# Forget-gate columns and indexer keys computed by feature and turned back; FoX's second log-forget product on the second key tile alone

## The chip, the cores and the metric

The program runs on one core of one Trainium2 chip, as one launch. The time is in device microseconds. The engines are TensorE (PE in the rows, with its weight loads as PEld), VectorE (DVE), ScalarE (ACT), GpSimd (POOL) and SyncE (SP), which issues most of the DMAs. Each engine works through its own instructions in order, and they wait for each other by semaphores.

## What is computed

A sequence of 256 tokens with 1024 features goes through two layers of a first block (feed-forward, a mixer of three kinds, cross attention to a memory, feed-forward) and then two layers of a second block (short convolution, sparse attention with an indexer, pooling, gates). What bears on this case is below.

```python
def first_block(...):                       # for each of DEPTH = 2 layers
    x = x + 0.5 * swiglu(rms_norm(x, ffn1_norm[l]), ffn1_w_in[l], ffn1_w_out[l])
    z = rms_norm(x, mix_norm[l]) @ mix_w_in[l]
    z_fox, z_moba, z_rwkv = jnp.split(z, [FOX_IN, FOX_IN + MOBA_IN], axis=-1)
...
def fox_mixer(z, f_bias, q_gain, k_gain):
    q, k, v, f = jnp.split(z, [FOX_WIDTH, 2 * FOX_WIDTH, 3 * FOX_WIDTH], axis=-1)   # f: 4 columns
    log_f = jax.nn.log_sigmoid(f + f_bias)
    # scores: q k^T / 8 + c[query] - c[key], c = cumsum(log_f) over tokens, causal, softmax
...
def rwkv7_mixer(z, ...):
    r, k, v, w_lo, a_lo, g_lo = jnp.split(zf, ...)       # low: 64 + 64 + 160 columns
    w_raw = w0 + jnp.tanh(w_lo) @ w2
    a = jax.nn.sigmoid(a0 + a_lo @ a2)
...
def sparse_attention_mixer(q, k, v, gate, iq, ik, iw, ...):  # second block
    iq = apply_rope(iq.reshape(B, S, IDX_HEADS, IDX_DIM), cos, sin)
    ik = apply_rope(ik[:, :, None, :], cos, sin)[:, :, 0, :]  # ik: 64 columns, iw: 8 columns
    score = einsum(relu(iq ik^T / 8), iw) / sqrt(8)           # picks top keys for each query
```

## The kernel before

**Weights.** All weights come in one stream of units of 128x1024 fp32 numbers (512 KB). SP loads unit u into one of four raw buffers as soon as VectorE has split unit u - 4. ScalarE (`act_split`, L315) rounds the unit to `whi`, once TensorE has used unit u - 4, and VectorE (`dve_split`, L324) writes the rest to `wlo`. TensorE multiplies each pair of operands in three matmuls (high by high, high by low, low by high), so one unit of 512 columns is 4 groups of 3 matmuls of 512 columns (`pe_unit`, L342 to L344), with the activations as the stationary operand and the weights moving: 128 tokens come out on partitions, features along the free axis. `pe_unit_turned` (L350) does it the other way: the weights are the stationary operand, all 256 tokens move, and the features come out on partitions.

**Mixer, low columns.** `pe_rw_low` works through four units. Of each, for two slices `kk` of 128 input features, `blocks` gives three outputs by feature (128, 96 and 64 partitions by 256 tokens, L367 to L369), and `beside` gives the four forget-gate columns by token (two tiles of 128 tokens by 4 columns, L362 to L364). ScalarE's `act_rw_low` then copies the three blocks to `LM` with a scale each (L884 to L886) and the 2x4 forget columns to `Z` (L887); VectorE's `dve_rw_low` adds the shifted tokens (L902). TensorE meanwhile does the first two units of group `z` 1, then `pe_rw_lora` (L928, L932), then two more, `pe_rw_cum`, and group 2.

**Forget gates.** `dve_at_tables` part 0 (L1507, L1509) prepares the gates, `act_at_tables` (L1522, L1524) takes the exponential and logarithm, part 1 the sign and factor. In `pe_at_scores`, FoX's logits of one head get one product for the queries and keys and then, for each token tile `st` up to the query tile, a product of the log gates `LN` (broadcast to 128 stationary columns) with the table `cum` (L1587). `cum` for `st` = 1 is zero for keys 0 to 127, since tokens of the second tile add nothing to the sums of the first.

**Second block.** `pe_block2` begins with the groups iq (four units), ik (one unit of 8 slices of 72 columns: 64 key columns and 8 head weights), k (four units). `pe_unit_keys` makes 72 columns by token in banks 2 and 0: per token tile 8 slices of 3 matmuls (L2360 to L2362). ScalarE's `act_group` scales them into `ikw` (L2374, L2375). VectorE turns iq and then ik by their angles (`dve_sp_index`, L2390 to L2398, L2411), with one `dve_split` between them, and TensorE's `pe_sp_index` transposes both (L745) behind the third unit of k. The groups take three pairs of banks in turn, each waiting for the copies of those before.

## Time and profile before

| | before |
|---|---|
| median of 3 runs | 1896.34 us |
| lowest, highest | 1893.74 us, 1907.27 us |
| the profiled execution | 1899.43 us |
| its span | 1898.1 us |
| TensorE busy | 1857.7 us (98%) |
| VectorE busy | 1165.2 us (61%) |
| ScalarE busy | 927.7 us (49%) |
| mean granted TensorE clock | 0.991 |

The span is the time from the first to the last recorded instruction; 1.3 us of the profiled execution lie around it. A matmul's row has its start and a modelled length; since matmuls overlap, what one costs is the distance from its start to the next one's start. The granted clock is 1.00 at 2.4 GHz and 0.50 at 1.2 GHz.

### The profile page before, as it was taken

How to read it: one execution, taken by the hardware profiler on the slowest of the kernel's cores; microseconds unless marked ns; L12 is line 12 of the kernel's file. 1: busy time of each engine (PE TensorE's matmuls, PEld its weight loads, DVE VectorE, ACT ScalarE, POOL GpSimd, SP SyncE). 2: the span in 40 equal slices, each digit the busy share in tenths (PEclk: the TensorE clock that was granted, in tenths of full speed). 3: DMA queues.
4: the chain of work that ended last, by engine and by line, in shares of the span. 5: the costliest groups of instructions: out<-in, count | busy, mean ns of one | idle time of the engine just before them, and what ended most of it. 6: DMA issues, size and time to landing. Idle time of an engine off the chain costs nothing.

```text
span 1898.1 us, 28284 instructions
## 1 busy us (share of the span) xinstructions
PE 1857.7 (98%) x11756; PEld 1565.4 (82%) x11756; DVE 1165.2 (61%) x1645; ACT 927.7 (49%) x1409; POOL 93.6 (5%) x59
## 2 busy tenths in 40 slices
PE   7999999999999999999999989999999999999999
PEld 6888888887888888888888878888888888888887
DVE  5555477765655565554677656555588548597556
ACT  5444474234544454445642355444455554556553
POOL 0000010040000000000100400000010000000000
PEclk9999999999999999999999999999999999999999
DMA  6655442023555566554420235655554456454454
GB/s 241 249 183 175 145 156 78 25 79 112 168 189 188 177 191 248 188 176 143 155 71 25 79 111 187 205 184 174 165 168 159 152 188 210 151 166 156 161 186 141
DMA packets 83616, 299.19 MB, mean 158 GB/s; under 512 B 9632, under 2 KB 10784, under 8 KB 83232
## 3 DMA queue, kind: packets, MB, share of 16 engines
q1 hardware_dynamic: 79328, 287.87, 45.8%
q10 hardware_dynamic: 3840, 8.03, 1.2%
q8 instruction: 93, 1.52, 0.3%
q0 software_dynamic: 320, 1.48, 0.2%
q14 instruction: 35, 0.29, 0.0%
HBM read 296.30 MB, written 1.05 MB: 157 GB/s over the span
## 4 chain that ended last, share of the span: by engine, by line
PE 94%; DVE 4%; issue 0%; ACT 0%; DMA 0%; POOL 0%; ACTq 0%; DVEq 0%
PE ps L342 24%; PE ps L344 24%; PE ps L343 24%; PE ps L367 2%; PE ps L369 2%; PE ps L368 2%; PE ps L808 1%; PE ps L1184 1%; PE ps L566 1%; PE ps L1187 1%; DVE wlo L324 1%; PE ps L2500 1%; PE ps L1175 1%; PE ps L1587 1%; PE ps L780 1%; DVE a_lo L420 1%
## 5 line engine op out<-in xcount | busy, mean ns | idle before, releaser
L324 DVE TENSOR_TENSOR wlo<-raw,whi 128x1024 fp32r<-128x1024 f32 (+1 forms) x546 | 663.3, 1222 | 423.0 <-ACT whi L315 422.0
L315 ACT ACTIVATE whi<-raw 128x1024 fp32r<-128x1024 f32 (+1 forms) x546 | 573.0, 1053 | 512.2 <-PE ps L344 468.2
L342 PE MATMUL ps<-whi,a_hi 128*128 128x512 f32 x1696 | 677.0, 399 | 5.8 <-DVE a_lo L1874 1.8
L344 PE MATMUL ps<-whi,a_lo 128*128 128x512 f32 x1696 | 663.8, 391 | 0.0
L343 PE MATMUL ps<-wlo,a_hi 128*128 128x512 f32 x1696 | 662.8, 391 | 0.0
L342 PEld LDWEIGHTS ps<-whi,a_hi 128*128 128x128 f32 x1696 | 320.2, 189 | 76.0 <-DVE a_lo L1874 2.3
L344 PEld LDWEIGHTS ps<-whi,a_lo 128*128 128x128 f32 x1696 | 319.7, 189 | 68.7
L343 PEld LDWEIGHTS ps<-wlo,a_hi 128*128 128x128 f32 x1696 | 320.5, 189 | 62.8
L342 PE MATMUL ps<-whi,h_hi 128*128 128x512 f32 x320 | 124.9, 390 | 0.0
L344 PE MATMUL ps<-whi,h_lo 128*128 128x512 f32 x320 | 124.6, 389 | 0.0
L343 PE MATMUL ps<-wlo,h_hi 128*128 128x512 f32 x320 | 124.5, 389 | 0.0
L367 PE MATMUL ps<-a_hi,whi 128*128 128x256 f32 (+2 forms) x304 | 88.7, 292 | 0.0
L369 PE MATMUL ps<-a_hi,wlo 128*128 128x256 f32 (+2 forms) x304 | 85.9, 282 | 0.0
L368 PE MATMUL ps<-a_lo,whi 128*128 128x256 f32 (+2 forms) x304 | 85.8, 282 | 0.0
L344 PEld LDWEIGHTS ps<-whi,h_lo 128*128 128x128 f32 x320 | 60.1, 188 | 12.5
L343 PEld LDWEIGHTS ps<-wlo,h_hi 128*128 128x128 f32 x320 | 60.1, 188 | 12.3
L342 PEld LDWEIGHTS ps<-whi,h_hi 128*128 128x128 f32 x320 | 60.1, 188 | 12.3
L588 ACT ACTIVATE arena<-ps,small 128x256 f32<-128x256 f32 x88 | 36.9, 470 | 67.2 <-PE ps L344 67.2
L631 DVE SCALAR_TENSOR_TENSOR arena<-ps,small,arena 128x256 f32<-128x256 f32 x88 | 38.5, 479 | 40.0 <-ACT arena L588 40.0
L497 POOL TENSOR_TENSOR small<-small,minus_half 128x2 f32<-128x2 f32 x10 | 7.0, 700 | 1057.3 <-DVE small L490 703.8
L367 PEld LDWEIGHTS ps<-a_hi,whi 128*128 128x128 f32 (+2 forms) x304 | 56.8, 187 | 0.7 <-issue 0.3
L368 PEld LDWEIGHTS ps<-a_lo,whi 128*128 128x128 f32 (+2 forms) x304 | 56.9, 187 | 0.2
(317 smaller groups left out, 1847.3 us busy)
## 6 DMA issues: line engine op xcount, KB each, us to landing
raw<-stream SPq DMA_DIRECT2D x546, 512.0 KB, 3.4
arena<-rows ACTq DMA_DIRECT2D x2, 1026.0 KB, 12.6
arena<-mem ACTq DMA_DIRECT2D x2, 1024.0 KB, 8.7
arena<-lora ACTq DMA_DIRECT2D x2, 768.0 KB, 6.1
arena<-rows ACTq DMA_DIRECT2D x2, 512.0 KB, 4.9
const_tables<-consts POOLq DMA_DIRECT2D x1, 901.0 KB, 4.9
arena<-band POOLq DMA_DIRECT2D x1, 544.0 KB, 4.0
x_res<-x SPq DMA_DIRECT2D x1, 512.0 KB, 3.7
```

What stands on the lines that cost most here:

```text
L315: self.split_hi.mark(act.activation(self.weights(self.whi, u), self.weights(self.raw, u), ACT.Copy), u)
L324: self.split_lo.mark(dve.tensor_tensor(self.weights(self.wlo, u), self.weights(self.raw, u), self.weights(self.whi, u).bitcast(F32), ALU.s ...
L342: pe.matmul(out, a_h, hi, start=start, stop=False, skip_group_check=True)
L343: pe.matmul(out, a_h, lo, start=False, stop=False, skip_group_check=True)
L344: last = pe.matmul(out, a_l, hi, start=False, stop=True, skip_group_check=True)
L367: pe.matmul(out, hi, self.AHI[:, kt, :], start=first and kt == 0, stop=False, skip_group_check=True)
L368: pe.matmul(out, hi, self.ALO[:, kt, :], start=False, stop=False, skip_group_check=True)
L369: last = pe.matmul(out, lo, self.AHI[:, kt, :], start=False, stop=True, skip_group_check=True)
L420: self.turned_lo.mark(dve.scalar_tensor_tensor(self.ALO[:, place, :], self.bank(banks[k % 4], S), gain[:, k:k + 1], self.AHI[:, place, :]. ...
L566: ins = pe.transpose(self.bank(banks[kk])[:, t * P:(t + 1) * P], self.h_buffer(j)[:, t, kk * P:(kk + 1) * P], self.c("ident"))
L588: self.silu.mark(act.activation(self.SG[:, t, :], self.bank((2 if j == 1 else 4) + t, 256), ACT.Silu, scale=self.rs(0, t)), key, j, t)
L631: self.h_ready.mark(dve.scalar_tensor_tensor(self.h_buffer(j)[:, t, :], self.bank((2 if j == 1 else 4) + t)[:, 256:512], self.rs(0, t), se ...
```

## The change

Three edits. The layouts of the weights in memory stay as they are.

1. The forget gates' four columns become rows 64 to 67 of the third block by feature (68 partitions instead of 64), and `beside` is gone. `act_rw_low` copies 68 rows to `LM`, the four with a scale of 1. Behind `pe_rw_lora` TensorE transposes the four rows back to tokens, for two tiles, and ScalarE copies them to `Z` behind the LoRA's sigmoids. VectorE's two small gate instructions stand behind `dve_at_norm`. Group 2 of `z` waits for the copy too.
2. In `pe_at_scores` the product for key tile `st` writes columns from `st` x 128 on alone.
3. The indexer's keys and head weights are computed by feature (72 partitions by 256 tokens in bank 3), copied to `sIKT` by ScalarE, transposed back by TensorE behind the first unit of k, and scaled into `ikw` by ScalarE behind one more split.

```diff
@@ -349,4 +349,3 @@
 
-    def pe_unit_turned(self, n, blocks, beside=()):
-
+    def pe_unit_turned(self, n, blocks):
@@ -358,8 +357,2 @@
             kt = 2 * n + kk
-            for out, c, w, first, t in beside:
-                hi, lo = self.whi[i][:, kk, c:c + w], self.wlo[i][:, kk, c:c + w]
-                a_h, a_l = self.AHI[:, kt, t * P:(t + 1) * P], self.ALO[:, kt, t * P:(t + 1) * P]
-                pe.matmul(out, a_h, hi, start=first and kt == 0, stop=False, skip_group_check=True)
-                pe.matmul(out, a_h, lo, start=False, stop=False, skip_group_check=True)
-                pe.matmul(out, a_l, hi, start=False, stop=True, skip_group_check=True)
             for out, c, w, first in blocks:
@@ -860,4 +853,3 @@
         self.pe_unit_turned(n, [(self.bank(0)[:, S:2 * S], 96, P, True), (self.bank(0)[0:96, 0:S], 0, 96, False),
-                                (self.bank(1)[0:64, 0:S], 224, 64, False)],
-                            [(self.bank(1)[:, S + 4 * t:S + 4 * t + 4], 288, 4, t == 0, t) for t in range(NT)])
+                                (self.bank(1)[0:68, 0:S], 224, 68, True)])
@@ -885,5 +877,3 @@
         m.mark(act.activation(M[:, 1, :], self.bank(0)[:, S:2 * S], ACT.Copy, scale=self.pv(PV_OML, 1)), "low", l, 1)
-        m.mark(act.activation(M[0:64, 2, :], self.bank(1)[0:64, 0:S], ACT.Copy, scale=self.pv(PV_OML, 2, 64)), "low", l, 2)
-        m.mark(act.activation(self.Z[:, :, ZF:ZF + 4], self.bank(1)[:, S:S + 8].rearrange("p (t h) -> p t h", t=NT),
-                              ACT.Copy), "forget", l)
+        m.mark(act.activation(M[0:68, 2, :], self.bank(1)[0:68, 0:S], ACT.Copy, scale=self.pv(PV_OML, 2, 68)), "low", l, 2)
         act.wait_ge(*self.rw_dve("low", l, 0))
@@ -897,3 +887,3 @@
         for i, w, src, need in ((0, 96, self.bank(0)[0:96, 0:S], ("low", l, 1)), (1, P, self.bank(0)[:, S:2 * S], None),
-                                (2, 64, self.bank(1)[0:64, 0:S], ("forget", l))):
+                                (2, 64, self.bank(1)[0:64, 0:S], ("low", l, 2))):
             if need is not None:
@@ -934,2 +924,6 @@
         self.rw_pe.mark(ins, "a", l)
+        for t in range(NT):
+            ins = pe.transpose(self.bank(1)[:, S + 4 * t:S + 4 * t + 4], self.LM[64:68, 2, t * P:(t + 1) * P],
+                               self.c("ident")[64:68, 64:68])
+        self.rw_pe.mark(ins, "forget", l)
@@ -943,2 +937,5 @@
             m.mark(act.activation(self.AT[:, i, :], self.half((6, 7), i), ACT.Sigmoid, bias=self.pv(PV_A0, i)), "a", l, i)
+        act.wait_ge(*self.rw_pe("forget", l))
+        m.mark(act.activation(self.Z[:, :, ZF:ZF + 4], self.bank(1)[:, S:S + 8].rearrange("p (t h) -> p t h", t=NT),
+                              ACT.Copy), "forget", l)
@@ -1586,4 +1583,4 @@
                 for st in range(qt + 1):
-                    ins = pe.matmul(out, self.LN[:, st, h:h + 1].to_broadcast([P, P]),
-                                    self.c("cum")[:, st * S:st * S + nk], start=False, stop=st == qt,
+                    ins = pe.matmul(out[:, st * P:nk], self.LN[:, st, h:h + 1].to_broadcast([P, P]),
+                                    self.c("cum")[:, st * S + st * P:st * S + nk], start=False, stop=st == qt,
                                     skip_group_check=True)
@@ -1943,3 +1940,3 @@
         pe, banks = self.nc.tensor, self.ZB[g]
-        for sem, value in {1: [], 2: [self.rw_dve("low", l, 2)], 3: self.z_done(l, 1)}[g]:
+        for sem, value in {1: [], 2: [self.rw_dve("low", l, 2), self.rw_act("forget", l)], 3: self.z_done(l, 1)}[g]:
             pe.wait_ge(sem, value)
@@ -2191,5 +2188,3 @@
         self.dve_rw_low(l)
-        self.dve_split(3)
-        self.dve_at_tables(l, 0)
-        self.dve_split(1)
+        self.dve_split(4)
         self.dve_z(l, 1)
@@ -2197,2 +2192,3 @@
         self.dve_at_norm(l, True)
+        self.dve_at_tables(l, 0)
         self.dve_split(1)
@@ -2320,3 +2316,3 @@
         first = 4 * g - 3 * (g > 1)
-        dst = self.ikw if name == "ik" else self.slot[name] if name in self.slot else self.mg[name[2]][name[1]]
+        dst = None if name == "ik" else self.slot[name] if name in self.slot else self.mg[name[2]][name[1]]
         return self.unit2(self.layer, "p") + first, ((2 * g) % 3, (2 * g + 1) % 3), dst
@@ -2333,3 +2329,3 @@
                 pe.wait_ge(*self.z_act1("p", l, self.GROUPS[g - 2]))
-            if g > 0:
+            if g > 0 and name != "k":
                 late = [self.z_act("p", l, self.GROUPS[g - 1])]
@@ -2340,3 +2336,3 @@
         if name == "ik":
-            self.pe_unit_keys(banks, late)
+            self.pe_unit_keys()
             return
@@ -2345,3 +2341,3 @@
 
-    def pe_unit_keys(self, banks, late):
+    def pe_unit_keys(self):
@@ -2350,16 +2346,32 @@
         pe.wait_ge(*self.split_lo(u))
-        hi, lo = self.weights(self.whi, u), self.weights(self.wlo, u)
-        for t in range(NT):
-            if t:
-                for sem, value in late:
-                    pe.wait_ge(sem, value)
-            out = self.bank(banks[t], 72)
-            for kt in range(8):
-                a_h, a_l = self.AHI[:, kt, t * P:(t + 1) * P], self.ALO[:, kt, t * P:(t + 1) * P]
-                h, low = hi[:, kt * 72:(kt + 1) * 72], lo[:, kt * 72:(kt + 1) * 72]
-                pe.matmul(out, a_h, h, start=kt == 0, stop=False, skip_group_check=True)
-                pe.matmul(out, a_h, low, start=False, stop=False, skip_group_check=True)
-                last = pe.matmul(out, a_l, h, start=False, stop=kt == 7, skip_group_check=True)
+        hi, lo, out = self.weights(self.whi, u), self.weights(self.wlo, u), self.bank(3)[0:72, 0:S]
+        for kt in range(8):
+            h, low = hi[:, kt * 72:(kt + 1) * 72], lo[:, kt * 72:(kt + 1) * 72]
+            pe.matmul(out, h, self.AHI[:, kt, :], start=kt == 0, stop=False, skip_group_check=True)
+            pe.matmul(out, h, self.ALO[:, kt, :], start=False, stop=False, skip_group_check=True)
+            last = pe.matmul(out, low, self.AHI[:, kt, :], start=False, stop=kt == 7, skip_group_check=True)
         self.unit_used.mark(last, u)
 
+    def act_keys(self, l):
+        act = self.nc.scalar
+        self.layer = l
+        act.wait_ge(*self.unit_used(self.group("ik")[0]))
+        self.sp_act.mark(act.activation(self.sIKT[0:72, :], self.bank(3)[0:72, 0:S], ACT.Copy), "ik", l)
+
+    def pe_keys_turn(self, l):
+
+        pe = self.nc.tensor
+        pe.wait_ge(*self.sp_act("ik", l))
+        for t in range(NT):
+            ins = pe.transpose(self.bank(3)[:, S + 72 * t:S + 72 * (t + 1)], self.sIKT[0:72, t * P:(t + 1) * P],
+                               self.c("ident")[0:72, 0:72])
+        self.sp_pe.mark(ins, "ik", l)
+
+    def act_keys_out(self, l):
+        act = self.nc.scalar
+        act.wait_ge(*self.sp_pe("ik", l))
+        for t, m in enumerate((self.z_act, self.z_act1)):
+            m.mark(act.activation(self.ikw[:, t, :], self.bank(3)[:, S + 72 * t:S + 72 * (t + 1)], ACT.Copy,
+                                  scale=self.rs(0, t)), "p", l, "ik")
+
     def act_group(self, l, name):
@@ -2369,3 +2381,3 @@
         func = ACT.Sigmoid if name[0] == "mg" else self.FUNCS[name] if name in self.FUNCS else ACT.Copy
-        act.wait_ge(*self.unit_used(unit + (0 if name == "ik" else 3)))
+        act.wait_ge(*self.unit_used(unit + 3))
         if name == "ag":
@@ -2846,4 +2858,6 @@
         self.pe_group(l, "ik", 0)
-        for n in range(3):
-            self.pe_group(l, "k", n)
+        self.pe_group(l, "k", 0)
+        self.pe_keys_turn(l)
+        self.pe_group(l, "k", 1)
+        self.pe_group(l, "k", 2)
         self.pe_sp_index(l)
@@ -2940,4 +2954,6 @@
         self.act_split(1)
-        self.act_group(l, "ik")
-        self.act_split(3)
+        self.act_keys(l)
+        self.act_split(1)
+        self.act_keys_out(l)
+        self.act_split(2)
         self.act_sp_index(l)
```

What TensorE does in the low columns, from the first unit on, is, before the change (L362 to L364 are the forget columns, L367 to L369 the blocks):

```order
L362 MATMUL ps<-whi,a_hi 128x4
L363 MATMUL ps<-wlo,a_hi 128x4
L364 MATMUL ps<-whi,a_lo 128x4
L362 MATMUL ps<-whi,a_hi 128x4
L363 MATMUL ps<-wlo,a_hi 128x4
L364 MATMUL ps<-whi,a_lo 128x4
L367 MATMUL ps<-a_hi,whi 128x256
L368 MATMUL ps<-a_lo,whi 128x256
L369 MATMUL ps<-a_hi,wlo 128x256
L367 MATMUL ps<-a_hi,whi 96x256
L368 MATMUL ps<-a_lo,whi 96x256
L369 MATMUL ps<-a_hi,wlo 96x256
```

and with the change, where the lines L360 to L362 are now those of the blocks:

```order
L360 MATMUL ps<-a_hi,whi 128x256
L361 MATMUL ps<-a_lo,whi 128x256
L362 MATMUL ps<-a_hi,wlo 128x256
L360 MATMUL ps<-a_hi,whi 96x256
L361 MATMUL ps<-a_lo,whi 96x256
L362 MATMUL ps<-a_hi,wlo 96x256
L360 MATMUL ps<-a_hi,whi 68x256
L361 MATMUL ps<-a_lo,whi 68x256
L362 MATMUL ps<-a_hi,wlo 68x256
L360 MATMUL ps<-a_hi,whi 128x256
```

The six matmuls of 4 columns are gone and the third block has 68 stationary columns.

At the keys of the second block, behind the last matmul of iq, TensorE has before the change 48 of these (here the first 6):

```order
L344 MATMUL ps<-whi,a_lo 128x512
L2360 MATMUL ps<-whi,a_hi 128x72
L2361 MATMUL ps<-wlo,a_hi 128x72
L2362 MATMUL ps<-whi,a_lo 128x72
L2360 MATMUL ps<-whi,a_hi 128x72
L2361 MATMUL ps<-wlo,a_hi 128x72
L2362 MATMUL ps<-whi,a_lo 128x72
```

and with the change 24 of these (here the first 4):

```order
L344 MATMUL ps<-whi,a_lo 128x512
L2350 MATMUL ps<-a_hi,whi 72x256
L2351 MATMUL ps<-a_lo,whi 72x256
L2352 MATMUL ps<-a_hi,wlo 72x256
L2350 MATMUL ps<-a_hi,whi 72x256
```

The moving operand went from 72 weight columns to 256 tokens. Between the first unit of k (12 matmuls, the last 3 here) and the second stands the turn with the change, two transposes of L2366; before, the two units followed each other directly:

```order
L342 MATMUL ps<-whi,a_hi 128x512
L343 MATMUL ps<-wlo,a_hi 128x512
L344 MATMUL ps<-whi,a_lo 128x512
L2366 MATMUL ps<-const_tables,arena 128x72 x2
L342 MATMUL ps<-whi,a_hi 128x512
```

Two transposes are added there, 12 matmuls of 512 columns behind the last of the keys.

ScalarE, from the copies of iq on, before the change:

```order
L2374 ACTIVATE arena<-ps,small 128x512
L2375 ACTIVATE arena<-ps,small 128x512
L315 ACTIVATE whi<-raw 128x1024
L2374 ACTIVATE arena<-ps,small 128x72
L2375 ACTIVATE arena<-ps,small 128x72
L315 ACTIVATE whi<-raw 128x1024 x3
L751 ACTIVATE arena<-ps 128x4x128 x2
```

and with the change, L2359 being the copy by feature and L2374 the two scaled copies by token:

```order
L2386 ACTIVATE arena<-ps,small 128x512
L2387 ACTIVATE arena<-ps,small 128x512
L315 ACTIVATE whi<-raw 128x1024
L2359 ACTIVATE arena<-ps 72x256
L315 ACTIVATE whi<-raw 128x1024
L2374 ACTIVATE arena<-ps,small 128x72 x2
L315 ACTIVATE whi<-raw 128x1024 x2
L744 ACTIVATE arena<-ps 128x4x128 x2
```

One of the three splits stands now between the first copy and the two others.

## Rows read from the trace of the kernel before

**Rows 1.** Page, parts 1 and 4: busy time by engine; chain by engine

```profile
PE 1857.7 (98%) x11756; PEld 1565.4 (82%) x11756; DVE 1165.2 (61%) x1645; ACT 927.7 (49%) x1409; POOL 93.6 (5%) x59
PE 94%; DVE 4%; issue 0%; ACT 0%; DMA 0%; POOL 0%; ACTq 0%; DVEq 0%
```

**Rows 2.** Waits of PE, whole span: line, what was waited for, total us, times, longest

```profile
PE ps L404 <- DMA x_res<-x: 9.5, 1, 9.5
```

**Rows 3.** Stretches of PE: us, busy (instructions), granted clock, DMA share, GB/s

```profile
208.16:222.04 13.88, 13.88 (x124) 1.00 0.36 115
870.87:884.75 13.88, 13.88 (x124) 1.00 0.34 115
1352.63:1358.37 5.74, 5.74 (x49) 0.92 0.72 221
1358.37:1364.39 6.02, 6.02 (x16) 0.51 0.41 139
1630.56:1637.61 7.05, 7.05 (x50) 0.74 0.70 214
1637.61:1640.97 3.36, 3.36 (x9) 0.54 0.05 18
```

**Rows 4.** Timeline of PE: start us, length us, line, tile, form, count

```profile
210.76 0.27 PE L368 MATMUL ps<-a_lo,whi 128*128 128x256 f32 x1
211.57 0.28 PE L369 MATMUL ps<-a_hi,wlo 128*64 128x256 f32 x1
...
279.25 0.28 PE L367 MATMUL ps<-a_hi,whi 128*128 128x256 f32 x1
283.21 0.28 PE L367 MATMUL ps<-a_hi,whi 128*128 128x256 f32 x1
```

**Rows 5.** Timeline of PE, narrow key matmuls, and 24 wide ones' first and last

```profile
222.04 0.40 PE L342 MATMUL ps<-whi,a_hi 128*128 128x512 f32 x1
227.28 0.40 PE L344 MATMUL ps<-whi,a_lo 128*128 128x512 f32 x1
...
1357.13 0.28 PE L2362 MATMUL ps<-whi,a_lo 128*128 128x72 f32 x1
1357.24 0.28 PE L2360 MATMUL ps<-whi,a_hi 128*128 128x72 f32 x1
```

**Rows 6.** Timeline of PE, four turns between feature-side matmuls

```profile
267.86 0.60 PE L745 MATMUL ps<-const_tables,arena 128*128 128x128 f32 x4
268.22 0.36 PE L367 MATMUL ps<-a_hi,whi 128*128 128x256 f32 x1
268.42 0.28 PE L368 MATMUL ps<-a_lo,whi 128*128 128x256 f32 x1
```

**Rows 7.** Timeline of PE in FoX's scores, first and second query tile

```profile
274.99 0.49 PE L1587 MATMUL ps<-const_tables,small 128*128 128x128 f32 x2
275.41 0.48 PE L1583 MATMUL ps<-arena 64*128 64x128 f32 x2
...
287.35 1.13 PE L1587 MATMUL ps<-const_tables,small 128*128 128x256 f32 x4
288.41 0.70 PE L1583 MATMUL ps<-arena 64*128 64x256 f32 x2
```

**Rows 8.** Timeline around block 2's keys, layer 0; in brackets idle before, releaser

```profile
1358.60 0.32 ACT L2374 ACTIVATE arena<-ps,small 128x72 f32<-128x72 f32 x1 [3.50 <-PE ps L2362]
1360.11 1.23 DVE L324 TENSOR_TENSOR wlo<-raw,whi 128x1024 fp32r<-128x1024 f32 x1
1362.31 0.36 DVE L2411 COPY small<-arena 128x128 f32<-128x128 f32 x2
1369.40 1.03 PE L745 MATMUL ps<-const_tables,arena 128*128 128x128 f32 x8
```

**Rows 9.** Timeline of ACT and DVE behind the LoRA step, layer 0

```profile
234.34 1.06 ACT L315 ACTIVATE whi<-raw 128x1024 fp32r<-128x1024 f32 x1 [1.42 <-PE ps L344]
244.36 1.23 DVE L324 TENSOR_TENSOR wlo<-raw,whi 128x1024 fp32r<-128x1024 f32 x1 [3.20 <-ACT whi L315]
```

## What the change does to the time: the prediction

> **What bounds the kernel now.** I read the page first: TensorE is busy for 1857.7 of 1898.1 us, and 94% of the chain that ended last is its own work, 4% VectorE's [rows 1]. The list of TensorE's waits comes next: its longest entry is the 9.5 us at the start for the load of x [rows 2], which no edit touches. So a microsecond of matmuls taken out is a microsecond of the end, as long as nothing that TensorE then meets earlier is late. What a matmul costs is therefore the distance between two starts, and I looked for it in the timeline, at every place that the change touches, and beside it at the granted clock of the same stretches. There the reader is to see two different things. In the low columns of both layers TensorE runs 13.88 us at a full clock [rows 3]. At the keys of the second block it stays busy throughout, and still the granted clock falls: 0.92 in the keys of layer 0 and 0.51 in the 6.02 us of wide matmuls behind them, 0.74 and 0.54 in layer 1 [rows 3]. The narrow key matmuls cost 0.11 us each at the full clock though they move only 72 columns [rows 5].
>
> **Part 1, the forget columns.** One layer's low stretch has eight slices of 15 matmuls: 6 of 4 columns and 9 of 256. The nine stay, one third of them with 68 stationary columns instead of 64. A 256-column matmul costs (211.57 - 210.76) / 7 = 0.116 us in this very stretch, with 64 to 128 stationary columns, and (283.21 - 279.25) / 33 = 0.120 us where all have 128 [rows 4]. I take 0.118: 72 of them are 8.50 us. The stretch shrinks from 13.88 by 5.38 us, in two layers by 10.8 us, with the two ends 10.5 and 11.1. The 48 removed per layer thus cost 0.112 us each, as much as one of 256 columns.
>
> What comes instead are two transposes per layer of 4 rows. The trace has no such small ones; the nearest are four of 128 columns: 0.36 us for four, and the next matmul's distance is 0.20 instead of 0.12 us [rows 6]. Two are 2 x 0.09 + 0.08 = 0.26 us. Low end nothing, since the next matmul may cover them, high end 0.6 us. They read what ScalarE and VectorE had to finish for the LoRA product directly ahead of them, so they wait for nothing new. The copy to Z moves on ScalarE behind the LoRA's sigmoids, where ScalarE then idles for 1.42 us before its next split [rows 9]; one small copy fits. VectorE's two gate instructions move behind the norm, where VectorE idles for 3.20 us [rows 9]. ScalarE's logarithm wants them only two splits later. Group 2 waits for the copy, but two units of weights and the cumulative sums lie between. I cost all this at nothing; if the cover were gone it would be the copy's own few tenths.
>
> The faster stretch also asks for weights sooner. A low unit is used up in 18 x 0.118 = 2.1 us instead of 3.5, and each use releases one split on ScalarE (1.06 us) and one on VectorE (1.23 us) [rows 9]. Both fit into 2.1 us, and the first unit of the next group is split 2.3 us behind the first low unit, when three low units, 6.4 us, are still to run. The transfers have room: the stretch uses 36% of the DMA engines [rows 3].
>
> **Part 2, FoX.** With 128 columns the log-gate product costs 275.41 - 274.99 = 0.42 us, with 256 columns (288.41 - 287.35) / 2 = 0.53 us [rows 7]. Four heads in two layers are 8 of them: 8 x 0.11 = 0.9 us. The lower end is 0, the upper one half of the wide product's cost, 8 x 0.265 = 2.1 us. I take the difference of the rows.
>
> **Part 3, the keys.** Now 48 narrow matmuls, then 24 of 256 columns with 72 stationary ones, 24 x 0.118 = 2.83 us. In layer 0 the keys take 5.74 us and the next 6.02 us hold the starts of 14 wide matmuls at half clock [rows 3] (the count in the row is 16 because two reach in). At the full clock a wide one costs (227.28 - 222.04) / 23 = 0.228 us [rows 5], 14 are 3.19 us. So 11.76 us become 2.83 + 3.19 = 6.02 and 5.7 us are saved. In layer 1 the keys take 7.05 and the next 8 wide ones 3.36 us [rows 3]; 10.41 become 2.83 + 1.82 = 4.65, again 5.8 us. Together 11.5 us. Of this 2 x (48 x 0.111 - 2.83) = 5.0 us is for fewer matmuls and 6.5 us for the clock. That the clock falls because of the narrow matmuls is my reading: both falls come during them, without any idle time. The low stretch, where the 4-column matmuls alternate with 256-column ones, keeps 1.00 [rows 3].
>
> The turn back is priced as above, 0.26 us per layer. It waits for ScalarE's copy of the keys. Layer 0 in the new order: keys end at 1352.6 + 2.8 = 1355.5, and the first unit of k keeps TensorE for 12 x 0.228 = 2.7 us. ScalarE is idle then (3.50 us before its old copy) [rows 8] and has 2.7 us for one copy, so I expect no wait. Behind the turn come two more units of k, and TensorE is at the index transposes at 1355.5 + 36 x 0.228 + 0.3 = 1364.0 instead of 1369.40 [rows 8]. It does 8 transposes of iq first (0.9 us) and then wants ik. VectorE's line does not move: it is at its split at 1360.11 and finishes ik at 1362.31 + 0.36 = 1362.7 [rows 8]. The slack before the ik transposes falls from some 7.6 to 2.2 us, but it stays. This is the step next in line to be late. Queued behind ScalarE's new wait for the turn are two splits, which need units of k that TensorE has not used by then anyway.
>
> **The sum.** 10.8 + 11.5 + 0.9 - 4 x 0.26 = 22.1 us. The profiled execution took 1899.43 us, so its like should take 1877.3 us. The median of the three runs, 1896.34, is 3.1 us lower; carried over, the forecast is 1874.2 us.
>
> **Rivals.** *The clock falls all the same.* The fall may belong to this place and not to the narrow matmuls. Then the 6.5 us stay and the gain is 15.6 us: 1880.7 us. Against it speaks that the other feature-side stretches hold the full pace (0.120 us through 33 distances) [rows 4]. Chance 0.12. The Trainium skill has such a rule, in "TensorE: Matmul & The Clock Gate", section "HAM oscillation": the clock is lost in idle gaps between bursts of matmuls. By that rule narrow matmuls without a gap lose nothing, and the trace disagrees, since the clock went to 0.51 with TensorE busy for all of the 6.02 us.
>
> *A wait takes the place of the work.* If VectorE's line at the keys ends later than I read, TensorE stands at the index transposes, and in the worst case arrives as late as now: 11.0 us of the gain go, 1885.2 us. It begins to count when VectorE is 2.2 us later. Against it: VectorE's chain there needs nothing later than before except ik itself. Chance 0.08.
>
> *Slower than before.* The new turned stretches or the arrival at new phases could bring further falls of the clock. One fall costs 6.02 - 3.19 = 2.8 us [rows 3]. It takes eight more of them than now to lose the 22.1 us, and 15 to be over 1% slower: 1915 us or more. For it speaks only that stationary blocks of 68 and 72 columns do not occur now in those stretches; those of 64 and 96 do, at full clock. Chance 0.02.
>
> **How the numbers follow.** The forecast has 0.78. Its own spread comes from the ends above (low columns ±0.3, FoX -0.9 to +1.2, turns -1.4 to +1.0), from falls of the clock elsewhere, of 2.8 us each, that may begin or end differently when all behind shifts, and from the three runs, which lie between 1893.74 and 1907.27. The range is 1868 to 1886 us: it takes in both smaller gains, and beyond it lie the last case and the tails. About 1% is what a measurement of this kernel can tell from no change; faster by over 1% means under 1877.4 us. The forecast is 3 us below that bound, so three quarters of its 0.78 count as faster, 0.58; the other quarter and the two smaller gains are within 1%, 0.40; slower has 0.02.
>
> **What would show it.** In the profile after: 72 matmuls in each low stretch in 8.4 to 8.7 us at clock 1.00; 24 key matmuls in 2.8 to 2.9 us and wide ones at 0.228 us behind them with clock 1.00, where now it falls; two turns at about 0.26 us each without idle time before them; 0.42 us for the second log-gate product; and no wait of TensorE at the index transposes. The prediction is wrong if the clock still falls behind the keys, if the 68- or 72-column blocks cost clearly over 0.12 us, or if new waits of several us stand in TensorE's list.

## The result, and the profile after

The changed kernel takes 1889.37 us (median of 11 executions, 1885.75 to 1892.29); the kernel before, timed beside it, 1904.02 us (1893.74 to 1908.95). The ratio is 0.9948, with a 95% interval of 0.9933 to 0.9964: faster by half a percent, within the 1% in which the prediction put 0.40. A repetition in a later session (e12) gave 0.9934 (0.9916 to 0.9953). The forecast of 1874.2 us was 15 us too low, and the result lies above its range. The medians differ by 14.7 us and the two profiled executions by 13.6 (1899.43 to 1885.86), where 22.1 were expected. The other half of the 15 us is the starting point: the forecast set out from 1896.34, the median of three executions of the kernel before, and the median of eleven is 1904.02.

Page of the kernel after, parts 1 and 4, and below it the first two entries of the list of waits of PE (line, what was waited for, total us, times, longest), against [rows 1] and [rows 2]:

```profile
PE 1844.4 (98%) x11620; PEld 1552.9 (82%) x11620; DVE 1164.7 (62%) x1645; ACT 928.3 (49%) x1411; POOL 93.6 (5%) x59
PE 94%; DVE 4%; issue 0%; ACT 0%; DMA 0%; POOL 0%; ACTq 0%; DVEq 0%
```

```profile
PE ps L397 <- DMA x_res<-x: 9.4, 1, 9.4
PE ps L839 <- DVE arena L832: 6.5, 2, 3.3
```

TensorE is busy for 13.3 us less, the chain is the same 94%, and no wait is new or longer. Now the places that the change touches. Stretches of PE of the kernel after (us, busy (instructions), granted clock, DMA share, GB/s): the low columns of both layers, the keys of layer 0, what follows them up to the index transposes, and the keys of layer 1 with what follows; against [rows 3]:

```profile
206.96:215.50 8.54, 8.54 (x76) 1.00 0.46 138
868.11:876.64 8.53, 8.53 (x75) 1.00 0.45 142
1350.21:1353.03 2.82, 2.82 (x25) 1.00 0.64 208
1353.03:1361.42 8.39, 8.39 (x40) 1.00 0.55 183
1625.30:1636.00 10.70, 10.70 (x56) 1.00 0.57 186
```

Timeline of PE, the two turns with the matmuls behind, and FoX's second query tile (start us, length us, line, tile, form, count), against [rows 6] and [rows 7]:

```profile
224.70 0.28 PE L926 MATMUL ps<-const_tables,arena 4*128 4x4 f32 x2
224.91 0.50 PE L342 MATMUL ps<-whi,a_hi 128*128 128x512 f32 x1
...
1355.77 0.29 PE L2366 MATMUL ps<-const_tables,arena 72*128 72x72 f32 x2
1355.86 0.48 PE L342 MATMUL ps<-whi,a_hi 128*128 128x512 f32 x1
1356.18 0.39 PE L343 MATMUL ps<-wlo,a_hi 128*128 128x512 f32 x1
```

```profile
281.02 0.92 PE L1584 MATMUL ps<-const_tables,small 128*128 128x256 f32 x4
281.87 0.70 PE L1580 MATMUL ps<-arena 64*128 64x256 f32 x2
```

All of it came as forecast: 8.54 us for 72 matmuls (8.50 expected), 2.82 for the keys (2.83), clock 1.00 behind them in both layers, 0.21 us for the forget turn, 0.09 + (0.32 - 0.23) = 0.18 for the keys' turn. FoX's pair of products takes 281.87 - 281.02 = 0.85 us for 1.06. So the gain was made, and something gave part of it back. Three stretches that ran at full clock before do not now:

```profile
321.00:327.80 6.80, 6.80 (x61) 0.50 0.00 0
368.80:372.20 3.40, 3.40 (x62) 0.50 0.04 14
942.20:955.90 13.70, 13.70 (x57) 0.50 0.00 1
```

The longest of them is in FoX's scores of the second query tile, layer 1. Timeline of PE there, before and then after; the two have the same instructions in the same order, but for the narrower second log-forget product of part 2. L1583 and L1587 of before are L1580 and L1584 of after:

```profile
949.44 0.70 PE L1583 MATMUL ps<-arena 64*128 64x256 f32 x2
950.06 1.13 PE L1587 MATMUL ps<-const_tables,small 128*128 128x256 f32 x4
```

```profile
940.53 1.08 PE L801 MATMUL ps<-arena 128*128 128x64 f32 x8
941.54 0.70 PE L1580 MATMUL ps<-arena 64*128 64x256 f32 x2
942.17 1.60 PE L1584 MATMUL ps<-const_tables,small 128*128 128x256 f32 x4
943.70 1.22 PE L1580 MATMUL ps<-arena 64*128 64x256 f32 x2
944.85 1.43 PE L1584 MATMUL ps<-const_tables,small 128*128 128x256 f32 x3
```

In after the first L1580 pair of this stretch still takes 942.17 - 941.54 = 0.63 us, as before (0.62); the next takes 944.85 - 943.70 = 1.15, with no idle time between the rows. The whole stretch, from the transposes of the first tile's probabilities through the spread of the lengths, before and then after, in both layers:

```profile
283.57:295.38 11.81, 11.81 (x87) 1.00 0.14 47
946.28:958.09 11.81, 11.81 (x87) 1.00 0.13 47
```

```profile
277.24:288.19 10.95, 10.95 (x86) 1.00 0.14 51
938.39:955.50 17.11, 17.11 (x87) 0.61 0.09 33
```

Layer 0 runs it at full clock and 0.86 us faster, which is part 2's work; layer 1 takes 17.11 us, 6.2 more than layer 0.

**One split for all runs.** Every execution has its span and its mean granted clock, and the low level is half of the full one. So span x (1 - clock) estimates the time lost to low clock, and span x clock the time that the same work takes at full clock. The estimate is good to about 2 us. The mean clock has three digits, which is 1 us, and the loss comes out a little too high: the stretch of the scores, 11.81 us at 1.00 and 18.15 at 0.62 (below), became 6.3 us longer, where the split says 18.15 x 0.38 = 6.9. It gives for the kernel before 1879.8 us of work and 20.5 us lost (mean of the 29 executions beside e1 to e4; 13 to 27 us lost), and for the changed kernel 1861.8 and 25.9 us (11 executions; 22.6 to 28.4).

In the other sessions the kernel before lost 16.6 to 21.3 us in the mean, with the same work within 0.5 us, so a difference in loss of a few us between sessions is not a finding. The work fell by 18.0 us and the loss rose by 5. The forecast had 15.6 us less work and 6.5 us less loss. Three executions stand apart and are left out of work and loss below, those of e3 and e14 of the medians too: one each of e2 (clock 0.936 at 1907.28 us, which by the split would be 122 us lost), e3 (10507.77 us) and e14 (3076.41 us); why they were so I do not know.

### The profile page after: what moved, and what is told of

Same layout as the page of the kernel before. It is cut to its first block, busy times and chain, and to the rows that moved or that the text cites. A ratio compares the mean times of both kernels' runs of the same rounds, so it can differ in the third digit from the quotient of the medians.

```text
span 1884.5 us, 28014 instructions
## 1 busy us (share of the span) xinstructions
PE 1844.4 (98%) x11620; PEld 1552.9 (82%) x11620; DVE 1164.7 (62%) x1645; ACT 928.3 (49%) x1411; POOL 93.6 (5%) x59
## 4 chain that ended last, share of the span: by engine, by line
PE 94%; DVE 4%; issue 0%; ACT 0%; DMA 0%; POOL 0%; ACTq 0%; DVEq 0%
PE ps L342 24%; PE ps L344 24%; PE ps L343 24%; PE ps L360 2%; PE ps L362 2%; PE ps L361 2%; PE ps L801 1%; PE ps L1181 1%; PE ps L559 1%; PE ps L1184 1%; DVE wlo L324 1%; PE ps L1172 1%; PE ps L1584 1%; PE ps L773 1%; PE ps L2512 1%; PE ps L1580 1%
## 5 line engine op out<-in xcount | busy, mean ns | idle before, releaser
L360 PE MATMUL ps<-a_hi,whi 128*128 128x256 f32 (+2 forms) x304 | 87.7, 288 | 0.0
L362 PE MATMUL ps<-a_hi,wlo 128*128 128x256 f32 (+2 forms) x304 | 85.9, 283 | 0.0
L342 PEld LDWEIGHTS ps<-whi,h_hi 128*128 128x128 f32 x320 | 60.1, 188 | 12.3
L360 PEld LDWEIGHTS ps<-a_hi,whi 128*128 128x128 f32 (+2 forms) x304 | 56.9, 187 | 0.9 <-issue 0.5
```

The source lines that it names most:

```text
L342: pe.matmul(out, a_h, hi, start=start, stop=False, skip_group_check=True)
L360: pe.matmul(out, hi, self.AHI[:, kt, :], start=first and kt == 0, stop=False, skip_group_check=True)
L362: last = pe.matmul(out, lo, self.AHI[:, kt, :], start=False, stop=True, skip_group_check=True)
```

## The experiments

All were timed in 5 rounds beside the kernel before. "Useless matmuls" are extra products of 512 columns into a bank that the next product starts afresh, at the head of the first wide unit behind the low columns; TensorE is at full clock there and each costs 0.23 us.

| run | what | median us | ratio to before (95%) | work us | lost us, mean (range) |
|---|---|---|---|---|---|
| after | the change | 1889.37 | 0.9948 (0.9933 to 0.9964) | 1861.8 | 25.9 (22.6 to 28.4) |
| e1_low | part 1 alone | 1902.67 | 1.0006 (0.9986 to 1.0026) | 1868.3 | 32.8 (24.6 to 40.0) |
| e2_fox | part 2 alone | 1902.98 | 0.9995 (0.9976 to 1.0014) | 1877.5 | 22.3 (9.4 to 24.7) |
| e3_keys | part 3 alone | 1888.69 | 0.9926 (0.9903 to 0.9949) | 1876.0 | 11.3 (in all five) |
| e4_narrow_back | change + narrow keys | 1904.29 | 1.0004 (0.9985 to 1.0023) | 1873.6 | 28.1 (22.7 to 32.4) |
| e5_fox_keys | parts 2 and 3 | 1885.57 | 0.9944 (0.9923 to 0.9965) | 1873.7 | 12.9 (9.4 to 22.7) |
| e6_low_keys_8 | parts 1 and 3, + 1.8 us | 1885.45 | 0.9928 (0.9907 to 0.9949) | 1868.8 | 15.1 (11.3 to 18.9) |
| e7_all_8 | change + 1.8 us | 1880.72 | 0.9902 (0.9881 to 0.9923) | 1867.0 | 12.9 (9.4 to 17.0) |
| e8_keys_7 | part 3 + 1.6 us | 1905.83 | 1.0038 (1.0023 to 1.0053) | 1877.5 | 26.8 (20.9 to 30.5) |
| e9_all_split | change, unit in the scores | 1882.77 | 0.9903 (0.9885 to 0.9922) | 1863.2 | 18.1 (15.0 to 18.8) |
| e10_keys_7_split | e8 with that unit | 1901.11 | 1.0002 (0.9989 to 1.0015) | 1876.6 | 22.8 (20.9 to 24.7) |
| e11_all_6 | change + 1.4 us | 1882.55 | 0.9896 (0.9869 to 0.9923) | 1866.0 | 13.8 (5.6 to 20.7) |
| e12_all_again | the change again | 1889.52 | 0.9934 (0.9916 to 0.9953) | 1862.0 | 25.2 (22.6 to 26.4) |
| e13_all_halves | change, unit in halves | 1886.07 | 0.9937 (0.9913 to 0.9961) | 1862.0 | 24.9 (20.7 to 30.3) |
| e14_all_quarters | change, unit in quarters | 1891.80 | 0.9955 (0.9938 to 0.9971) | 1861.9 | 28.7 (26.4 to 32.2) |
| e15_all_6_halves | e11 with halves | 1884.57 | 0.9916 (0.9898 to 0.9935) | 1865.2 | 18.2 (15.0 to 20.7) |
| e16_before_halves | before, with halves | 1897.70 | 0.9983 (0.9968 to 0.9998) | 1880.4 | 15.8 (13.2 to 20.9) |
| e17_all_two_units | change, two units | 1887.81 | 0.9917 (0.9892 to 0.9943) | 1867.9 | 17.9 (15.1 to 20.8) |
| e18_all_8_split | e7 with e9's unit | 1881.58 | 0.9888 (0.9860 to 0.9915) | 1867.5 | 13.2 (9.4 to 15.1) |

### The parts apart

Each kernel has the hunks of one part of the diff shown ahead and no other. Expected:

> The forget columns by feature alone (part 1), the keys and FoX as before. Theory A (the clock's falls in the mixer come and go with the moment of the execution, whatever the kernel): the stretch is 5.3 us shorter in each layer, two turns cost 0.2 us each, so the work is 10.2 us less and the ratio is near 0.9946; falls in the mixer appear in some executions of both kernels. Theory B (the earlier arrival of TensorE in the mixer makes the falls seen in the profile after at 321, 369 and 942 us): they come with this part, cost it up to 12 us, and the ratio is 0.998 to 1.001.

> FoX's second product on 128 columns alone (part 2). The profile after shows 0.85 us for the two products of a head instead of 1.06, so 8 x 0.21 = 1.7 us less and a ratio of 0.9991 under both theories; theory B allows new falls, theory A none that the kernel before would not have.

> The keys by feature alone (part 3). Both theories: no fall of the clock at the keys. If each execution of the kernel before has both falls there, 5.0 us of work, 6.5 us of clock and 0.3 us of turns make a ratio near 0.9941; if the falls at the keys come in only some executions, it is between 0.9941 and 0.9975. Nothing in the mixer changes under theory B, so the mixer's falls are those of the kernel before.

Part 1 removed 11.5 us of work and won no time: its loss is 12.3 us above before's. Part 2 alone is within the measurement of no change: 2.3 us less work and 1.8 more loss, both about what the split can tell. Part 3 alone is as fast as the whole change or faster, with 14.2 us more work and 14.6 us less loss. The stretch of the scores, part 1 and then part 3:

```profile
277.52:295.67 18.15, 18.15 (x87) 0.62 0.08 30
945.98:964.14 18.16, 18.16 (x87) 0.62 0.08 30
```

```profile
283.61:295.42 11.81, 11.81 (x87) 1.00 0.15 49
946.43:958.24 11.81, 11.81 (x87) 1.00 0.14 49
```

Same instructions, 18.15 us at 0.62 and 11.81 us at 1.00. In all four stretches in the traces of part 2 and parts 2 and 3 it ran at 1.00 too. The falls in the scores thus come with part 1, which does not touch these instructions. That is theory B of what was expected, whose times e1 met too (1.0006 in 0.998 to 1.001); theory A had 0.9946.

### The narrow key matmuls again

The whole change, with the 48 removed products put back as useless ones behind the new keys:

```diff
+        for t in range(NT):
+            out = self.bank(3)[:, S:S + 72]
+            for kt in range(8):
...
+                pe.matmul(out, a_h, h, start=kt == 0, stop=False, skip_group_check=True)
+                pe.matmul(out, a_h, low, start=False, stop=False, skip_group_check=True)
+                last = pe.matmul(out, a_l, h, start=False, stop=kt == 7, skip_group_check=True)
         self.unit_used.mark(last, u)
```

> The whole change, and behind the keys by feature the 48 narrow matmuls of before once more, as extra work whose result is not used. If narrow matmuls make the clock fall: falls are back behind the keys in both layers, and the time is 2 x (5.3 + 3.3) = 17 us above that of the whole change (ratio near 1.004 to the kernel before). If the fall belonged to something else at that place, the clock stays at 1.00 there and only 10.7 us are added (ratio near 1.0005).

```profile
1353.03:1360.70 7.67, 7.67 (x64) 1.00 0.63 199
1360.70:1367.50 6.80, 6.80 (x25) 0.50 0.03 10
```

(Stretches of PE, e4_narrow_back, then part 3 alone:)

```profile
1350.00:1364.00 14.00, 14.00 (x76) 1.00 0.45 149
```

With the narrow products the clock is back at 0.50 for 6.8 us in layer 0 and for 3.4 in layer 1 (from 1643.96 us), without them it stays. The time alone would have said otherwise: 1.0004 is the ratio expected with no fall (1.0005), not the 1.004 expected with falls. The work rose by 11.8 us, about the 96 x 0.11 = 10.6 us of the products, but the loss only from 25.9 to 28.1 us in the mean. In the profiled execution the 5.1 us lost at the keys stand beside shorter falls elsewhere, 10.2 us at low clock in the scores of layer 1 for 13.7.

The other traces settle it. Narrow key matmuls stand in those of before, e1, e2, e4 and e16, two stretches each, and in 9 of these 10 a fall of 3.4 or 6.8 us begins during them or at most 0.7 us behind them. The tenth, layer 1 of e1, keeps the clock:

```profile
1636.24:1641.60 5.36, 5.36 (x50) 1.00 0.75 209
```

In the 15 traces with the keys by feature and no narrow ones, at as many positions, none of the 30 stretches has a fall. That bears out the reading in the prediction: the fall comes with the narrow matmuls and not with the place, though not every time.

### Moved, with nothing else changed

Two theories were left for the scores: something in part 1 brings the falls (theory C in what was expected), or only where TensorE's stream stands when it reaches the scores (theory P). The 5.3 us that part 1 takes out ahead of them shift it. So the next kernels shift the stream by useless matmuls alone, `more` being 8, 7 or 6:

```diff
-            pe.matmul(out, a_h, hi, start=start, stop=False, skip_group_check=True)
+            for _ in range(more if n == 0 else 0):
+                pe.matmul(out, a_h, hi, start=True, stop=True, skip_group_check=True)
+            pe.matmul(out, a_h, hi, start=start, stop=False, skip_group_check=True)
```

> Parts 2 and 3 without part 1. Work at full clock: the span of part 3 alone less half of its time at low clock was 1875.8 us; less 1.7 for FoX gives 1874. Theory P (the falls of the clock in the mixer depend on where TensorE's stream stands when the clock can fall, and part 1 moved the stream by 5.3 us in each layer): without part 1 no fall in the second tile's scores (about 283 and 947 us). Part 2 moves the stream by 1.7 us behind them, and part 2 alone had falls at 327 and 375 us: with them about 1897, without them about 1886. Theory C (part 1's own content brings the falls): no fall in the scores either, and the same two times; this run is there for the time.

> Parts 1 and 3, and 8 useless matmuls of 512 columns (8 x 0.23 = 1.8 us, at full clock) at the head of the first wide unit behind each low stretch, so that part 1 moves TensorE's stream by 3.5 us there instead of 5.3. Nothing is left out. Theory P: the second tile's scores stand where they do not fall (against the last fall of the same layer they would lie as in the kernel before, give or take 0.1 us): no fall at about 279 and 941 us, some 23 us at low clock in all, work of 1875.8 - 12.8 + 3.6 = 1866.6, so a span of about 1878. Theory C: the low stretches and all behind them hold what they held before, so the falls of 10 to 14 us in the scores stay in both layers: about 1890.

> The whole change and the same 8 useless matmuls in each layer. Work 1861.5 + 3.6 = 1865 us. Theory P: no fall in the second tile's scores; the falls at about 321 and 369 us, which part 2 alone had too, may stay: 1877 without them, 1889 with them and their like in layer 1. Theory C: falls in the scores of both layers as well: 1889 to 1895.

> Part 3 alone, in the place of part 1 nothing but 7 useless matmuls of 512 columns (1.6 us) behind each low stretch, in which every 4-column matmul stays. Part 3 alone was 1889.0 us with 22.7 us at low clock and no fall in the scores. Theory P: moved later by 1.6 us the scores come to stand where they stood in the runs with part 1: falls of 7 to 14 us in one or both layers at about 287 and 951 us, a time of 1896 to 1905. Theory C: the falls belong to part 1, which is not in this kernel: 3.2 us more work and no new fall, 1892.

> The whole change with 6 useless matmuls (1.4 us) for 8. Work 1861.5 + 2.7 = 1864.2. In the run with 8 the scores of layer 0 fell where they began 77.4 us behind the layer's first fall; with 0.45 us less they begin at about 76.9, where the runs so far show none. Theory P: fewer executions with a fall in the scores: a median of 1877 to 1880. Rival (it is chance from run to run): the same spread as with 8, 1880 less 0.9.

> The changed kernel as it is, on the chip of the runs beside it: 0.995 of the time before, 1886 to 1892 us, with a fall in the second tile's scores of at least one layer.

The scores' stretch in e8_keys_7, which has no part 1, and in e6_low_keys_8, which has it:

```profile
285.31:303.51 18.20, 18.20 (x87) 0.62 0.09 31
957.53:975.73 18.20, 18.20 (x87) 0.62 0.09 30
```

```profile
280.15:291.95 11.80, 11.80 (x86) 1.00 0.15 46
939.57:951.37 11.80, 11.80 (x86) 1.00 0.14 47
```

Useless work of 3.2 us made part 3's kernel slower by 1.1% of the time before, 0.9926 to 1.0038, the loss going from 11.3 to 26.8 us; and 3.6 us of it made the whole change faster, 0.9948 and 0.9934 to 0.9902, the loss going from 25 to 12.9 us. So the falls are not part 1's content. Its shift is enough to bring them and another shift takes them away. The rival fell in both directions. As for the times, e5 (1885.57 for 1886) and e8 (1905.83, just above 1896 to 1905) came about as expected, e7 (1880.72) lies between its 1877 and 1889, e6 had its 22.7 us at low clock in the profiled execution (23 expected) but a median of 1885.45 for 1878, and e11 has 1882.55 for 1877 to 1880. The theory tells where a fall can come, and does not give the time to better than some 7 us.

With 8 the scores of layer 0 still fell in the profiled execution (e7, below, first row), with 6 in neither layer (e11):

```profile
279.69:295.35 15.66, 15.66 (x87) 0.67 0.11 36
944.58:955.53 10.95, 10.95 (x86) 1.00 0.15 50
```

```profile
279.09:290.04 10.95, 10.95 (x86) 1.00 0.16 50
934.40:945.35 10.95, 10.95 (x87) 1.00 0.16 51
```

But among e11's six executions the loss goes from 5.6 to 20.7 us (1873.82 to 1887.57 us), so a shift moves the odds and does not fix them.

What counts for the stretch can be read from the traces as its distance from the end of the layer's first fall, which lies around TensorE's wait for L832 (L839 before); its end is read in stretches of 0.1 us. The stretches that hold wide matmuls (e9 and later, but for e11 and e12) are not in it. Over the uncut stretches of all traces (e11's layer 1 has no such fall):

| distance, us | stretches | fell |
|---|---|---|
| 70.7 to 71.9 | e1 (both layers), e4 (both), after and e12 (layer 1) | 6 of 6 |
| 72.2 to 73.6 | after and e12 (layer 0), e6 (both), e7 (layer 1), e11 (layer 0) | 0 of 6 |
| 74.0 | e7 (layer 0) | 1 of 1 |
| 75.9 to 77.1 | before, e2, e3, e5 (both layers each) | 0 of 8 |
| 77.6 to 77.8 | e8 (both) | 2 of 2 |

Between neighbours that differ by 0.3 to 0.5 us the outcome changes. The table was made after the runs, and no run was planned to test it. Part 1 moved the stretch from the fourth row to the first two.

### Wide matmuls among the short ones

The other question was whether order can cure what position brings. `pe_rw_cols(l, 2, (4, 5))`, 24 wide matmuls of 2.8 us, stood behind the spread; it is issued inside the scores:

```diff
         for h in range(4):
+            if between is not None and h == 2:
+                between()
...
-        self.pe_at_scores(l, True, 1)
+        self.pe_at_scores(l, True, 1, between=lambda: self.pe_rw_cols(l, 2, (4, 5)))
         self.pe_rw_spread(l)
-        self.pe_rw_cols(l, 2, (4, 5))
```

e13, e15 and e16 issue half of it ahead of head 0 and half ahead of head 2, e14 a quarter ahead of each head, e17 the whole unit ahead of head 0 and `pe_rw_cols(l, 3, (4, 5))` ahead of head 2.

> The whole change, and FoX's scores of the second tile cut in two: the third unit of the key columns (24 wide matmuls of 256 columns, 2.8 us, which stood behind the spread of the lengths) is issued between head 1 and head 2. No work is added or left out. Theory P': the stretch of some 12 us of short fp32 matmuls is what falls, and where it stands decides whether it does; with wide matmuls in its middle it does not fall wherever it stands: no fall from 277 to 300 and from 938 to 960 us, work of 1861.5 us, and 1873 us if only the falls of part 3 alone are left, 1881 with the falls at 321 and 369 us. The scores end 2.8 us later for ACT and DVE; the transposes of their probabilities (L773) have about that much slack, so at most 1 us of wait in each layer. Rival: what falls is set by what lies ahead of the stretch, and the fall comes as before, at 1887 to 1890.

> Part 3 alone with the 7 useless matmuls (1905.8 us, falls of 13.7 us in the scores of both layers), and the scores cut in two as in the whole change's run. Theory P': work stays at 1879 us, both falls in the scores go, at most 30 us at low clock are left: 1890 to 1895. Rival: the falls stay and the time with them, 1903 to 1908.

> The whole change, with the third unit of key columns cut into halves of 12 wide matmuls (1.4 us each): one ahead of head 0 of the second tile's scores, one between heads 1 and 2. No work added. With the whole unit between heads 1 and 2 the falls in the scores were 6.8 us for 13.7, both in the part ahead of the unit. If what falls is a long row of short fp32 matmuls without wide ones among them (theory P'), the part ahead now holds 3.1 and 3.3 us of them with wide ones between: no fall from 277 to 284 and from 938 to 945 us, at most one of 3.4 behind, 1873 to 1879 us. Rival (the stretch's mean counts, not how the wide ones are spread): falls of 6.8 us or more stay, 1882 as with the whole unit.

> The same in four pieces of 6 wide matmuls (0.7 us), one ahead of each head. Theory P': as with halves or better, 1873 to 1879. Rival: 1882 or more.

> The halves with the 6 useless matmuls (1.4 us) in each layer. The 6 alone: 1873.8 to 1887.6 us, 10.2 us at low clock in its profiled execution. Position and cut are independent if theory P' holds: work 1864.2 + 5 to 12 lost, 1870 to 1878, and a narrower spread than with the 6 alone. Rival: the halves move the later stretches to a place where they fall, 1880 or more.

> The kernel before with the halves alone. It has no fall in the scores, so theory P' gives it nothing there: 0.998 to 1.002 of the time before, with the falls of 6.8 us at the keys of block 2. Rival (the halves are worth something by themselves, by less waiting or a better order): 0.995 or less, and then the gains of the runs with halves say nothing on the falls.

> The whole change, with whole units of key columns (24 wide matmuls, 2.8 us, each): the third ahead of head 0 of the second tile's scores, the fourth between heads 1 and 2. Theory S (a fall comes where short fp32 matmuls hold long enough, and only a solid block of wide ones, not a sprinkling, keeps the clock up): the parts of short ones are now some 3, 3.3 and 5.3 us long, so no fall or one of 3.4 us in each layer's scores. The transposes of the probabilities now come up to 2.5 us before their exponentials are done in each layer, so up to 5 us more idle: work of 1861.5 to 1867, with 10 to 17 us lost 1873 to 1883. Rival (order does not matter, position alone does): 10 us or more at low clock in the scores of both layers, over 1886.

> The whole change with both what helped: 8 useless matmuls (1880.7 us alone) and the whole unit between heads 1 and 2 (1882.8 alone). If they add up, falls in the scores are rare and short: work 1865, 11 to 15 us lost, 1876 to 1880, and a range under 5 us. If position alone decides, moving the spread and all behind the split by nothing leaves 1880 to 1882; if the split moves the later stretches to a worse place, over 1883.

The stretches now hold the 24 (e17: 48) wide matmuls too. e9_all_split, e14_all_quarters and e18_all_8_split:

```profile
277.16:294.09 16.93, 16.93 (x110) 0.80 0.10 33
938.58:955.48 16.90, 16.90 (x110) 0.80 0.10 33
```

```profile
277.46:291.31 13.85, 13.85 (x110) 1.00 0.12 41
938.65:960.29 21.64, 21.64 (x110) 0.61 0.08 26
```

```profile
280.05:293.88 13.83, 13.83 (x111) 1.00 0.13 40
938.64:952.46 13.82, 13.82 (x110) 1.00 0.14 42
```

My expectation for e9 and e10 was that no fall would be left; 6.8 us in each layer were, for 13.7 in the uncut stretches that fell. The time gained is real (0.9903; e10 against e8 1.0002 for 1.0038), half of what I hoped.

For e10 the traces show where it comes from, 27.3 us at low clock in the scores of e8 and 13.7 in e10. For e9 they do not: the scores of the change have 13.7 us in layer 1 and none in layer 0, those of e9 6.8 in each, the same sum, and its profiled execution has its 6.5 us less at low clock in the falls behind (one of 3.4 us near 324 us for 6.8 and 3.4 near 321 and 369). How much of e9's gain is the block and how much the new position of what follows is not shown.

The halves and quarters were meant to do better and did not: e13 is at 0.9937, e14 at 0.9955, both nearer to their rivals' 1882 or more than to the 1873 to 1879 hoped for. And e15, halves with 6 useless matmuls, is at 1884.57 us where 1870 to 1878 were expected and its rival said 1880 or more. In e14's layer 1 the fall begins as the first piece ends and lasts through the three others, 21.64 us at 0.61, with 17.1 us at low clock. In e9 the block begins at 285.65 and the clock is back 1.2 us later (stretches of PE):

```profile
285.00:286.00 1.00, 1.00 (x5) 0.50 0.00 0
286.00:287.00 1.00, 1.00 (x6) 0.55 0.00 0
287.00:288.00 1.00, 1.00 (x11) 1.00 0.00 0
```

So one solid block ended a fall and the same matmuls in four pieces did not. Position does not explain this: in layer 1 the stretch begins 71.2 to 71.4 us behind the first fall in all of these, and it has 13.7 us at low clock uncut (after, e12), 6.8 with the block (e9), 10.2 with the halves (e13) and 17.1 with the quarters (e14), one profiled execution each. Two solid blocks (e17) left one fall of 3.4 us in each layer's scores, and it lay inside the first block, whose 24 matmuls took 286.20 - 281.66 = 4.5 us instead of 2.8. TensorE then waited for the probabilities, as its price said it might, and the clock fell once more at that wait (timeline of PE, then the entry of its waits):

```profile
281.66 0.36 PE L360 MATMUL ps<-a_hi,whi 128*128 128x256 f32 x1
286.20 0.70 PE L1582 MATMUL ps<-arena 64*128 64x256 f32 x2
...
299.73 1.09 PE L1537 MATMUL ps<-const_tables,arena 128*128 128x128 f32 x4 [2.79 <-DVE arena L1030]
```

```profile
PE ps L1537 <- DVE arena L1030: 5.6, 2, 2.8
```

Its expectation allowed up to 5 us of that; 5.6 came, and at 1887.81 us, where 1873 to 1883 were expected, the run gains nothing over e9. e16 gives the kernel before 0.9983, so the order by itself is worth at most a little there. Shift and block together (e18) have the lowest ratio, 0.9888, but its interval overlaps those of e7, e9 and e11, and 1881.58 us is what was expected if position alone decides (1880 to 1882). Its scores stand 73.2 and 73.3 us behind the first fall, where the uncut ones did not fall either, so it says nothing on the block.

**The best version.** e7, e9, e11 and e18 all beat before by about 1.0 to 1.1% and the change by 0.3 to 0.6% (e9 and e12, in one session: 0.9903 and 0.9934, intervals that overlap). I would take e9: it contains no useless work, and its five executions (1880.59 to 1883.45) all lie below all six of the change in the same session (1885.23 to 1890.55).

## Why the prediction was wrong

- **Low columns, 10.8 us: right.** 2 x 5.34 = 10.7 us in the rows; 11.5 by part 1's work (with the turn), where 10.3 were forecast, within what the split can tell.
- **The keys, 5.0 us of work and 6.5 of clock: right.** Part 3 alone has 3.8 us less work (4.5 forecast with its turns). It lost 5.7 us less than before between the two profiled executions (17.0 and 11.3) and 9 in the mean (20.5 and 11.3). Where the other executions of before lost more their mean clock does not tell.
- **FoX, 0.9 us: under-sized, inside its bound of 2.1.** The pair became 0.21 us shorter per head, not 0.11: 2 x 0.86 = 1.7 us in the stretches' rows; the 2.3 by part 2's work are within what the split can tell. The shortened product costs 0.85 - 0.53 = 0.32 us behind a 256-column one; the 0.42 I took is its cost in the first tile, where other instructions surround it.
- **Turns, copies, the index transposes, the weights: right.** 0.21 and 0.18 us for 0.26; ScalarE's copy was done in time, the transposes began at 1361.42 with no wait, and the longest waits are the old ones.
- **The step that failed** is the sum's silence on the clock outside the touched places. "Falls of the clock elsewhere, of 2.8 us each, that may begin or end differently when all behind shifts" stood in the range alone, with a mean of zero. The slower rival, "the arrival at new phases could bring further falls of the clock", named the mechanism and got 0.02, because it would take eight of them to be slower. What happened is between: with part 1, 12 us more were lost in the mean than before (32.8 for 20.5), of which part 3 gave 9 back; the 2 that part 2 seems to cost are not shown. In the sum a term of +12 us belonged beside part 1, or at least an even chance of it. The price of a fall was too low as well: 2.8 us, read from the wide matmuls behind the keys alone, where a fall in the scores cost 17.11 - 10.95 = 6.2 us. The trace offered a sign that I did not use: the second tile's scores are 11.81 us of short matmuls, unsplit (one fp32 product where the units have three of high and low parts), without a unit of wide ones among them, and the key stretches had just shown that TensorE can lose the clock without idling.
- **The starting point, 1896.34 us, was low by chance.** Its three executions were 1893.74, 1896.34 and 1907.27 us, and the median of eleven, 1904.02, is 7.7 us higher; in the other sessions the median of the kernel before was 1896.39 to 1902.53. The gain fell short by 7.4 us, and the starting point makes the rest of the 15. Even with the whole gain of 22.1 us the changed kernel would have been at 1882, inside the range but not at 1874.
- **The rival "the clock falls all the same", 1880.7 us, 0.12**, had the right sign for the wrong place. At the keys the clock held.

The Trainium skill's page "TensorE: Matmul & The Clock Gate", section "HAM oscillation", blames idle gaps between bursts. The prediction already set the keys against it. The scores disagree too: 17.11 us with TensorE busy for all 17.11, at 0.61. One fall in each layer does go with an idle gap: the first begins within about 1.3 us of the end of TensorE's 3.3 us wait for L832, in 39 of the 40 layers traced.

What stays open: why a shift of 0.3 to 0.5 us decides, and what decides the falls at 321 us (small matmuls and transposes, with waits of up to 1.5 us among them) and at 369 us. The traces of after, e1, e2, e12 and e14 have their like, 43 to 51 and 91 to 99 us behind the start of the scores, those of before, e3, e5 and e6 have neither in layer 0. I did not isolate them.

## What to carry to other kernels

Before a cut is credited with its microseconds, look behind it for stretches of some microseconds (here 5.7 for the keys, 11.8 for the scores) in which TensorE runs only narrow or short, unsplit matmuls: they may be at full clock by their position alone, and a cut ahead of them shifts them. Split each execution's time into span x clock and span x (1 - clock), compare kernels in both, and if the second rises while the first falls, try a shift of 1 to 2 us or a solid block of wide matmuls inside the stretch before giving up the cut. And when executions of one kernel spread by 15 us, as here, forecast the difference to the kernel before, not the time: a median of three moves by several us.

## What the runs showed of the hardware

- The granted clock fell to its lower level, 1.2 GHz, with TensorE busy throughout. The uncut scores ran at 1.00 in 15 stretches and at 0.61 to 0.67 in 9, with the same instructions but for part 2's columns.
- 3.2 us of useless dense matmuls cost 17 us between the medians of e3 and e8, 21 by the ratios (0.9926 to 1.0038); 3.6 us of them in another kernel saved 6 to 9 (0.9934 and 0.9948 to 0.9902).
- A stationary block of 72 columns with 256 moving ones cost 2.82 us for 24, 0.118 each, where blocks of 128 cost 0.116 to 0.120. Moving operands of 4 and of 72 columns cost 0.11 us each, nearly as much as 256 columns.
- A fall came during or just behind 9 of 10 stretches of narrow key matmuls, and at none of the 30 of the same keys by feature.
- Six wide matmuls at a time between short ones did not end a low stretch (e14, 21.64 us at 0.61). Behind 24 in one block the clock was back after 1.2 us (e9), yet a fall could also begin inside such a block (e17).
